# Attention outputs of a two-layer encoder step: the second subtraction of the low half moved from VectorE to ScalarE and GpSimd, the last addition one chunk later

## The reference, cut to what matters

```python
sc = (q @ k^T) * scale (+ forget terms in layer 1)       # masked
pr = softmax(sc)                                         # per head, fp32
o  = pr @ v                                              # (rows, 64) per head
y  = o.reshape(rows, 16 * 64) @ w_o                      # w_oa / w_ob
```

## Time and profile before

| what | value |
|---|---|
| median of 3 runs | 3232.65 us (3231.03 to 3233.51) |
| the profiled execution, its own time | 3237.43 us |
| its span | 3235.5 us |
| granted TensorE clock, mean | 0.968 of full |
| TensorE matmul busy | 3021.0 us (93%) |
| VectorE busy | 2036.1 us (63%) |
| GpSimd busy | 1449.0 us (45%) |
| ScalarE busy | 977.5 us (30%) |
| first attention, about | 291 to 601 us |
| second attention, about | 1858 to 2162 us |

### The profile page before, as it was taken

The page is one execution under the profiler, slowest core; times in us unless marked ns, Lnnn a source line. Parts: engine busy times, 40 slices in busy tenths (PEclk is TensorE's granted clock), DMA queues, the critical chain, the costliest instruction groups (busy, mean ns, idle before and its releaser), DMA issues.

```text
span 3235.5 us, 54355 instructions
## 1 busy us (share of the span) xinstructions
PE 3021.0 (93%) x18978; PEld 2913.1 (90%) x18978; DVE 2036.1 (63%) x3680; ACT 977.5 (30%) x2191; POOL 1449.0 (45%) x943
## 2 busy tenths in 40 slices
PE   7999999998999999998879999889899999999987
PEld 6889888888999999997878988889899999999877
DVE  5657888465655655657574588864655665655664
ACT  3234777332000000004342167753300000000242
POOL 5223555464333333436564455544543343343563
PEclk9999999998999999999998999999899999999998
DMA  3397544211111111111102565621011111111111
GB/s 110 137 326 243 140 121 120 101 40 44 41 52 44 41 51 45 40 51 53 40 20 100 186 148 132 146 80 66 33 53 39 45 52 39 45 52 39 62 38 54
DMA packets 163114, 264.62 MB, mean 82 GB/s; under 512 B 95040, under 2 KB 108880, under 8 KB 162624
## 3 DMA queue, kind: packets, MB, share of 16 engines
q1 hardware_dynamic: 163008, 263.21, 26.2%
HBM read 197.74 MB, written 65.42 MB: 81 GB/s over the span
## 4 chain that ended last, share of the span: by engine, by line
PE 77%; DVE 9%; issue 5%; ACT 4%; POOL 2%; DMA 2%; SPq 1%; DVEq 0%; ACTq 0%; POOLq 0%
PE ps L1302 30%; PE ps L1011 12%; PE ps L1012 12%; PE ps L1013 12%; PE ps L1210 3%; PE ps L1186 3%; DVE sublayer_out L2018 1%; DVE act_lo L2033 1%; PE ps L1158 1%; DVE neg_max L2184 1%; DVE out_partial L2209 1%; PE ps L1032 1%; PE ps L1046 1%; PE ps L1159 1%; ACT probs_t_hi L1651 1%
## 5 line engine op out<-in xcount | busy, mean ns | idle before, releaser
L843 POOL TENSOR_TENSOR weight_hi<-weight_raw,ones 128x1024 fp32r<-128x1024 f32 x185 | 365.8, 1977 | 1184.4 <-PE ps L1013 593.8
L2252 DVE TENSOR_TENSOR sublayer_out<-ps,sublayer_out 128x352 f32<-128x352 f32 x1008 | 527.6, 524 | 518.3 <-PE ps L1013 509.7
L1302 PE MATMUL ps<-act_hi,weight_hi 128*128 128x352 f32 x2112 | 686.5, 325 | 10.0 <-ACT ffn_act L1699 4.8
L1302 PE MATMUL ps<-act_hi,weight_lo 128*128 128x352 f32 x2112 | 684.3, 324 | 0.0
L1302 PE MATMUL ps<-act_lo,weight_hi 128*128 128x352 f32 x2112 | 684.2, 324 | 0.0
L1011 PE MATMUL ps<-act_hi,weight_hi 128*128 128x352 f32 (+2 forms) x1392 | 476.5, 342 | 50.0 <-POOL weight_lo L848 20.0
L848 POOL TENSOR_TENSOR weight_lo<-weight_raw,weight_hi 128x1024 fp32r<-128x1024 f32 x197 | 485.4, 2464 | 38.5 <-ACT weight_hi L1689 24.0
L1013 PE MATMUL ps<-act_hi,weight_lo 128*128 128x352 f32 (+2 forms) x1392 | 461.8, 332 | 0.0
L1012 PE MATMUL ps<-act_lo,weight_hi 128*128 128x352 f32 (+2 forms) x1392 | 461.7, 332 | 0.0
L910 POOL TENSOR_TENSOR probs<-probs,row_inv 128x1024 f32<-128x1024 f32 (+8 forms) x288 | 311.1, 1092 | 323.1 <-DVE row_inv L2192 322.0
L1302 PEld LDWEIGHTS ps<-act_hi,weight_hi 128*128 128x128 f32 x2112 | 399.4, 189 | 14.0 <-issue 6.9
(11 more groups left out here) (171 smaller groups left out, 5774.3 us busy)
## 6 DMA issues: line engine op xcount, KB each, us to landing
weight_raw<-units SPq DMA_DIRECT2D x201, 512.0 KB, 3.2
k_hi<-kB_hi SPq DMA_DIRECT2D x32, 328.0 KB
qA_hi<-stage_hi SPq DMA_DIRECT2D x16, 528.0 KB, 3.5
qA_lo<-stage_lo SPq DMA_DIRECT2D x16, 528.0 KB, 4.6
q_hi<-qA_hi SPq DMA_DIRECT2D x16, 528.0 KB
q_lo<-qA_lo SPq DMA_DIRECT2D x16, 528.0 KB
kA_hi<-stage_hi SPq DMA_DIRECT2D x8, 656.0 KB, 3.0
kA_lo<-stage_lo SPq DMA_DIRECT2D x8, 656.0 KB, 4.7
```

The costliest lines, as they stand in the source:

```text
L843: pool.tensor_tensor(wh[:, slot, :], wraw[:, slot, :], ones[:, 0:1].to_broadcast((P, UW)), ALU.mult).then_inc(w_hi[slot], 1)
L1302: mm = nc.tensor.matmul(ps[:, 3 * slot + b, 0:TB], a, x, start=(k == 0 and pas == 0), stop=(k == KD - 1 and pas == 2))
L2252: V.tensor_tensor(y[:, m, c], src, y[:, m, c], ALU.add).then_inc(f_acc, 1)
```

## The change

The subtraction is taken apart. ScalarE, right after it has copied `act_hi`, copies the product with V-low from PSUM to `out_partial`; this is one more activation for each part and a wait for `at_olo` of the part before. GpSimd subtracts `act_hi` from `out_partial` in place, ahead of the `normalise` of the step in which the chunk falls; it waits for its own `normalise` before, for ScalarE's copy (`at_ocopy`) and for its own result (`at_oadd`). VectorE only adds, one chunk later (`LATE_LAG = 3`), and waits for `at_oadd`. GpSimd's loop over pairs gets the first pair written out and a drain of three parts, which stands ahead of `tail_pool`'s unit 0.

```diff
-PV_LAG, OUT_LAG = 2, 2
+PV_LAG, OUT_LAG, LATE_LAG = 2, 2, 3
...
+        def out_sum(c):
+            rows = slice(64 * (c // HC % 2), 64 * (c // HC % 2) + VD)
+            return osum[rows, 0:DEC if last_tile(c) == 8 else 512]
...
             def normalise(layer):
                 base_n = layer * H * STEPS
-                with pool.Fori(0, H // 2) as i:
-                    for s in range(PAIR):
+                def outs(i, c, s, first):
+                    if is_out(c):
+                        dst, _, n = out_part(c, i, nh)
+                        if s >= 1 or not first:
+                            pool.wait_ge(at_p, i * PAIR + (base_n + s))
+                        pool.wait_ge(at_ocopy, i * 6 + (3 * layer * H + n))
+                        pool.tensor_tensor(out_sum(c), out_sum(c), dst.bitcast(F32), ALU.subtract).then_inc(at_oadd, 1)
+                        pool.wait_ge(at_oadd, i * 6 + (3 * layer * H + n))
+                def pair(i, first, drain=False):
+                    for s in range(DRAIN if drain else PAIR):
+                        for c in chunks_at(s):
+                            if c >= OUT_LAG or not first:
+                                outs(i, c - OUT_LAG, 0 if drain else s, first)
...
+                pair(0, True)
+                with pool.Fori(1, H // 2) as i:
+                    pair(i, False)
+                pair(H // 2, False, True)
...
                         nc.scalar.activation(dst, src, ACT.Copy).then_inc(at_ohi, 1)
+                        if not (isinstance(i, int) and i == 0 and n == 1):
+                            act.wait_ge(at_olo, i * 6 + (3 * layer * H + n - 1))
+                        nc.scalar.activation(out_sum(c), src_lo, ACT.Copy).then_inc(at_ocopy, 1)
...
                         dst, src, n = out_part(c, i, nl)
-                        dve.wait_ge(at_ohi, i * 6 + (3 * layer * H + n))
...
-                        V.tensor_tensor(part, src_lo, out_part(c, i, nh)[0].bitcast(F32), ALU.subtract).then_inc(at_oadd, 1)
                         dve.wait_ge(at_oadd, i * 6 + (3 * layer * H + n))
-                        V.tensor_tensor(dst, src, part, ALU.add).then_inc(at_olo, 1)
+                        V.tensor_tensor(dst, src, out_sum(c), ALU.add).then_inc(at_olo, 1)
...
-                            if c >= OUT_LAG or not first:
-                                outs(i, c - OUT_LAG)
+                            if c >= LATE_LAG or not first:
+                                outs(i, c - LATE_LAG)
```

More of the change, by code:

```diff
@@ L471, in build_program @@
                                             sem("at_pt_lo"), sem("at_o_lo"))
-        at_oadd = sem("at_o_lo_added")
+        at_oadd, at_ocopy = sem("at_o_lo_added"), sem("at_o_low_copied")
         at_e, at_hi, at_ohi = sem("at_exp"), sem("at_pt_hi"), sem("at_o_hi")
@@ L903, in normalise @@
                 base_n = layer * H * STEPS
-                with pool.Fori(0, H // 2) as i:
-                    for s in range(PAIR):
+                def outs(i, c, s, first):
[11 more added lines that the diff above has]
+                                outs(i, c - OUT_LAG, 0 if drain else s, first)
+                        if drain:
+                            continue
                         k, tile = s % STEPS, ORDER[s % STEPS]
@@ L911, in normalise @@
                                            ALU.mult).then_inc(at_p, 1)
+                    if drain:
+                        for c in range(-OUT_LAG, 0):
+                            outs(i, c, 0, False)
+                pair(0, True)
+                with pool.Fori(1, H // 2) as i:
+                    pair(i, False)
+                pair(H // 2, False, True)
             normalise(0)
@@ L1656, in outs @@
                         dst, src, _ = out_part(c, i, nh)
+                        _, src_lo, n = out_part(c, i, nh, 1)
                         act.wait_ge(at_pv, i * (2 * HC) + (base_c + c + 1))
                         nc.scalar.activation(dst, src, ACT.Copy).then_inc(at_ohi, 1)
+                        if not (isinstance(i, int) and i == 0 and n == 1):
+                            act.wait_ge(at_olo, i * 6 + (3 * layer * H + n - 1))
+                        nc.scalar.activation(out_sum(c), src_lo, ACT.Copy).then_inc(at_ocopy, 1)
                 def pair(i, first, drain=False):
@@ L2222, in pair @@
                                 lo(i, c)
-                            if c >= OUT_LAG or not first:
-                                outs(i, c - OUT_LAG)
+                            if c >= LATE_LAG or not first:
+                                outs(i, c - LATE_LAG)
                     if drain:
-                        for c in range(-OUT_LAG, 0):
+                        for c in range(-LATE_LAG, 0):
                             outs(i, c)
```

## The result

The changed kernel took 3245.36 us, the median of 6 runs (3239.18 to 3247.38); the kernel before took 3231.73 us beside it (6 runs, 3225.4 to 3233.51). The ratio is 1.0041 with a 95% interval of 1.0031 to 1.0052: **slower by 0.41%, 13.6 us**. The forecast was 3219 us in a range of 3200 to 3238, so the time lies 7 us above the range and on the other side of no change.

What follows compares the result with a forecast made beforehand. TensorE, busy 93% of the span, was taken as the bound. Attention heads gain 24 us and the two attention ends lose 10, so 3232.65 - 14 = 3219 us (-0.43%), range 3200 to 3238 us.

Steps and rivals of the forecast that it cites:

- TensorE's wait for exponentials in layer 0: Scores' weight loads in the first attention: their wait would fall from 13.1 to under 4 us in 14 heads.
- the advance of the 768-column maximum: VectorE in a head: tile 5's row maximum would start at 408.52 instead of 410.06, 1.54 us earlier.
- GpSimd's 1.23 us for the subtraction: Each 64x512 subtraction moved to GpSimd would take 1.23 us, between bounds of 0.69 and 2.46.
- the addition's wait for GpSimd: VectorE's addition in the attention loops would wait around 0.3 us for GpSimd's result, 28 times in each loop.
- the two ends: End of each attention: GpSimd's drain delays the split of projection unit 0, 5 us per layer, 10 us in all.
- the sum in a head: Net gain per attention head: 0.8 us in layer 0, 0.7 in layer 1, 24 us over 16 heads each.
- the single stall shown above: TensorE's 1.03 us idle before the scores at 412.09 in a layer 0 head, which would go whole.
- the forecast's three signs of being wrong: GpSimd's subtraction nearer 2 us; ScalarE's copy delaying exponentials more than high halves; attention ends not 5 us longer each.
- the slower rival: GpSimd's subtraction, over about 2.0 us from copy to semaphore, holds up VectorE; attention gains nothing: 3243 us, chance 0.14.
- the second rival: The attention stall moves and the ends eat the rest: -10 + 10 = 0, 3233 us; chance 0.20.
- The full gain: First rival: TensorE becomes the bound everywhere, attention waits go; 3198 us, a gain beyond 29 us, chance 0.16.
- the ceiling's 56 us: All attention waits removed: 1.34 us a head in layer 0 and 2.19 in layer 1, over 16 heads each.

Runs made afterwards that it cites:

- the short versions: Changed kernel with GpSimd's subtraction, ScalarE's copy, or both cut to 32 columns, the rest left out: 3223.22, 3222.29 and 3205.93 us.
- this case's test kernel: Kernel before plus ScalarE's copy, VectorE subtracting all three parts from the copied tile at lag 2: 3298.88 us, ratio 1.021.
- the other kernel with a copy: Kernel before plus ScalarE's copy, VectorE subtracting only the two 512-column parts from it, the 32-column part from PSUM: 3274.08 us, ratio 1.0141.

## Why the prediction was wrong

**What held.** TensorE's wait for exponentials in layer 0, which went; the advance of the 768-column maximum (1.66 us from the start of its scores, 1.54 forecast); GpSimd's 1.23 us for the subtraction (1284 ns); ScalarE's 0.6 us for a copy (594 ns); the addition's wait for GpSimd (0.35 us on average, 21 and 27 times in 14 heads); and above all the two ends: +5 us each was forecast, the idle time grew by 5.03 and 5.04 us, and taking the split out of it returned 7 us.

**The step that failed is the sum in a head**, "0.8 us for layer 0" and "0.7 us for layer 1", 24 us in all. Measured, a head of layer 0 gained nothing (a pair went from 38.02 to 38.09 us), and a head of layer 1 lost 0.2 us (36.91 to 37.34 a pair). With 14 pairs in the loops that is about 0.5 + 3.0 us of loss where 24 of gain were entered. With the ends' 10 us and 2.7 us more at the end of layer 1, where TensorE ran at half clock (granted 0.50, 1.2 GHz) from 2150 to 2155 us as it had not before (1.00), this comes to 16 us, the 15.9 us of the profiled attentions within rounding. That the half clock makes all of the 2.7 us is not shown.

**Why it failed.** The steps before it had the parts. They followed VectorE to the addition, put a wait of 0.3 us there (0.45 in the head shown), and left the maximum of tile 4 an advance of "0.5"; measured from the start of tile 5's scores, it came 407.80 - 403.38 = 4.42 us later instead of 411.58 - 406.90 = 4.68 before, an advance of 0.26 us out of 1.54. The sum then credited 0.8 us all the same, "because a good part of the waits is the single stall shown above". That a stall of the scores is gone is no gain as long as the next thing that TensorE needs, the low half behind that maximum, comes hardly earlier. What was left after it, 0.49 us in the head shown, went at two more places: 0.2 us around the second large copy, for which the prediction had allowed up to 0.6, and 0.3 us behind the 32-column copy, for which its sum had no term. The right reading was in the earlier trace rows: what the move is worth is the advance of the last instruction on VectorE before TensorE's next wait, not of the first. The kernel before with lag 3 alone shows it without GpSimd: the same exchange of waits, and 0.19% slower. Two of the forecast's three signs of being wrong did not come: GpSimd's subtraction was not near 2 us, and the ends were 5 us longer each. The third, whether ScalarE's copy delays exponentials by more than high halves, was not measured. Its range was also drawn against its chances: it left a tenth beyond 3238 us and gave the slower case, at 3243 us, 0.14.

**Which cost is which.** The place of VectorE's last instruction decides, and who subtracts only then matters:

| us, median | VectorE's last instruction at lag 2 | lag 3 | lag 4 |
|---|---|---|---|
| VectorE subtracts and adds | 3231.7 | 3237.1 | 3217.2 |
| ScalarE, GpSimd and VectorE, unit 0 split early | not run | 3238.3 | 3203.7 |

At lag 3 the hand-over is worth nothing (1 us): VectorE's relief is spent on the waits for copy and subtraction, which the short versions give back. At lag 4 it is worth 13.5 us more than the place alone. Two things go with that: those waits lie behind what TensorE needs, and the matmuls' 10.8 us of waiting for `act_lo` in layer 0, which VectorE's two late instructions cause in the kernel before at lag 4, are gone. How the 13.5 us divide between them is not shown. At lag 3 the subtraction (22 us) and the copy (23 us, both 39) are each a large part of the loss; at lag 4 the wait of the addition for GpSimd is gone in layer 0 and the place of the copy is worth too little for the medians to show. The rule of the Trainium skill that the prediction weighed (GPSIMD Engine Reference, section "Engine selection") holds for the time on the engine, 1284 ns against 694, but it does not settle the move: the same slow subtraction stands in both cells of the lower row.

**The rivals.** The time is that of the slower rival, 3243 us with a chance of 0.14, and so is the place, the addition in front of tile 4's maximum. Its threshold was wrong: it asked for about 2.0 us from copy to semaphore and a wait of 1 us. In the head shown the addition starts 1.62 us after the copy's end (405.47 to 407.09), 1.28 of them on GpSimd, and waits 0.45. That wait, the addition's own 0.68 us and ScalarE's copies together did what I had asked of the wait alone. The mechanism is rather that of the second rival, "the stall moves", with nothing left of the 10 us that it gave the attentions. The full gain, beyond 29 us, was not within reach at lag 3: with both new pieces of work on 32 columns the changed kernel is 26 us below the kernel before. The kernel that drops the subtraction and pays nothing for it gave 35 of the ceiling's 56 us.

**Layer 1's clock** rose to 1.00 as the ceiling's side of the forecast allowed, and yet its pairs became longer. Single forms of matmuls are shorter at the full clock (281 ns instead of 287 for a transpose, 332 instead of 343 for the product of a high half with V), while the waits of the weight loads grew by 6 us. How much longer layer 1 would have been at 0.97 was not measured. Why the copy's effect is larger in layer 0 (1.35 us a pair for it, 0.87 for the subtraction) while in layer 1 they are equal stays open too.

## What to carry to other kernels

On engines that work in order, ask of a moved instruction what stands behind it in its new place and who waits for that; here one chunk later cost 6 us and two chunks later gained 13, for the same work on the same engines, and in the changed kernel the second chunk alone brought 36 us. When a stall disappears, credit only what the next wait does not take back, and follow the chain to the next thing that the bounding engine needs, through the whole head and with the small pieces of work in it. Work hidden at the end of a phase, such as the weight split, is queued behind whatever is added to that drain: put it ahead explicitly.

## What the hardware showed that was not expected

A VectorE instruction with both inputs and its output in SBUF did not get through beside a running GpSimd one: the 64x32 subtraction took 1319 ns in the mean of 32 instead of 194 ns with one input in PSUM, and it ended 0.03 to 0.05 us after GpSimd's 128x1024 multiplication in each of the 31 that the timeline lists. The Trainium skill states this in SBUF — State Buffer, section "SBUF: two separate sides": VectorE with two SBUF inputs and GpSimd reading SBUF lock the shared ports against each other for a whole instruction. The trace agrees, and it cost this case's test kernel some 25 us. With one input in PSUM the same subtraction stands at the same place in the other kernel with a copy, and runs through in the middle of GpSimd's multiplication (406.32 to 408.22 us):

```profile
406.98 0.20 DVE L2214 TENSOR_TENSOR out_partial<-ps,act_hi 64x32 f32<-64x32 f32 x1
```

The mean of the 64x512 form, 705 ns beside 694 from PSUM, hides the same effect, because nearly all of these ran while GpSimd stood idle or had under 0.2 us left. The last one of each attention did not: it began beside GpSimd's split of a weight (629.65 to 631.54 us) and took 1.25 us instead of 0.69.

```profile
630.84 1.25 DVE L2214 TENSOR_TENSOR out_partial<-out_partial,act_hi 64x512 f32<-64x512 f32 x1 [2.45 <-ACT out_partial L1663]
```

The change itself shows nothing of it; its addition has one input in PSUM (683 ns, 684 before).
